# Moving two transposition steps and one wait inside the down product of a mixture-of-experts kernel

## What is computed

```
def swiglu(h, w_gu, w_down):
    gate, up = jnp.split(h @ w_gu, 2, axis=-1)
    return (jax.nn.silu(gate) * up) @ w_down

def moe_swiglu(h, router_w, w_gu, w_down):
    ...
    for e in range(N_EXPERTS):          # 8 experts, D_FF_E = 1408
        y = y + gates[..., e:e + 1] * swiglu(h, w_gu[e], w_down[e])
```

## Time and profile before

| | |
|---|---|
| median of 3 runs | 2287.32 us (2282.84 to 2290.6) |
| profiled execution | 2283.95 us, its span 2282.1 us |
| PE busy | 2029.0 us (89%) |
| DVE, ACT, POOL busy | 958.3, 725.9, 772.2 us |
| dense SwiGLU (layer 0) on PE | 873 to 1361 us |
| expert SwiGLU (layer 1) on PE | 1478.95 to 2224.6 us |
| HBM read, written | 284.45 MB, 32.65 MB |

### The profile page before, as it was taken

One profiled execution on the slowest core, in us unless ns is written; L12 is line 12 of the kernel. 1 busy time (PEld: TensorE's weight loads), 2 busy tenths in 40 slices (PEclk: granted clock), 3 DMA queues, 4 the chain that ended last, 5 costly groups with the idle time before them and its releaser, 6 DMA issues. The chain is left out here.

```text
span 2282.1 us, 38499 instructions
## 1 busy us (share of the span) xinstructions
PE 2029.0 (89%) x14354; PEld 1532.4 (67%) x14355; DVE 958.3 (42%) x1618; ACT 725.9 (32%) x1193; POOL 772.2 (34%) x474
## 2 busy tenths in 40 slices
PE   4998999999998798999999989399999899899990
PEld 2545776777676546878788867367776677677870
DVE  3203665666566355423222247353333433432226
ACT  0112332333233102222122201164445545544331
POOL 0006224422443112212121233275355645543324
PEclk7899999999999899999999998599999999999995
DMA  7113233223321514224322421586658758765344
GB/s 252 56 37 105 79 106 124 80 72 104 124 80 62 198 52 153 93 88 137 99 94 85 162 92 56 185 279 213 188 184 264 245 181 255 247 197 171 106 162 152
DMA packets 257563, 320.58 MB, mean 140 GB/s; under 512 B 25417, under 2 KB 197713, under 8 KB 257323
## 3 DMA queue, kind: packets, MB, share of 16 engines
q1 hardware_dynamic: 242315, 285.01, 39.0%
q10 hardware_dynamic: 10976, 17.49, 2.2%
q0 software_dynamic: 4032, 14.68, 1.8%
HBM read 284.45 MB, written 32.65 MB: 139 GB/s over the span
## 5 line engine op out<-in xcount | busy, mean ns | idle before, releaser
L1301 POOL TENSOR_TENSOR wlo<-wring,whi 128x1024 fp32r<-128x1024 f32 x182 | 461.0, 2536 | 781.7 <-ACT whi L1733 711.6
L1109 PE MATMUL pp<-whi,xTh 128*128 128x512 f32 (+1 forms) x1152 | 449.7, 390 | 37.5 <-issue 11.6
L1733 ACT ACTIVATE whi<-wring 128x1024 fp32r<-128x1024 f32 (+1 forms) x328 | 318.8, 980 | 454.8 <-PE pp L1111 375.2
L1111 PE MATMUL pp<-wlo,xTh 128*128 128x512 f32 (+1 forms) x1152 | 434.0, 377 | 0.0
L1110 PE MATMUL pp<-whi,xTl 128*128 128x512 f32 (+1 forms) x1152 | 433.6, 376 | 0.0
L2295 DVE TENSOR_TENSOR wlo<-wring,whi 128x1024 fp32r<-128x1024 f32 x182 | 227.3, 1249 | 229.4 <-ACT whi L1733 141.9
L1109 PEld LDWEIGHTS pp<-whi,xTh 128*128 128x128 f32 x1152 | 220.4, 191 | 93.3 <-issue 28.7
L1111 PEld LDWEIGHTS pp<-wlo,xTh 128*128 128x128 f32 x1152 | 219.9, 191 | 40.4
L1110 PEld LDWEIGHTS pp<-whi,xTl 128*128 128x128 f32 x1152 | 220.8, 192 | 34.9
L1109 PE MATMUL pp<-whi,hTh 128*128 128x512 f32 x528 | 212.7, 403 | 8.5 <-DVE ybuf L2251 3.9
L728 PE MATMUL pp<-xT,wring 128*128 128x512 f32 x384 | 206.5, 620 | 2.6 <-ACT scratch L1534 2.0
(11 more groups left out here) (291 smaller groups left out, 2675.0 us busy)
## 6 DMA issues: line engine op xcount, KB each, us to landing
wring<-in_moe_w_gu SPq DMA_DIRECT2D x320, 256.0 KB, 3.8
wring<-in_ada_w SPq DMA_DIRECT2D x80, 512.0 KB, 4.8
wring<-in_moe_w_down SPq DMA_DIRECT2D x160, 256.0 KB, 3.5
wring<-in_ffn_w_gu SPq DMA_DIRECT2D x80, 256.0 KB, 3.1
wring<-in_dn_w_in SPq DMA_DIRECT2D x96, 128.0 KB, 3.4
wring<-in_ffn_w_down SPq DMA_DIRECT2D x40, 256.0 KB, 3.0
expert_in<-zeros SPq DMA_DIRECT2D x36, 256.0 KB, 3.3
wring<-in_ada_w SPq DMA_DIRECT2D x32, 256.0 KB, 5.2
```

Of the source, the lines that this page charges most:

```text
L1109: pe.matmul(out, hi[:, c0 + c, tt], wh, start=(first and c == 0), stop=False)
L1111: mm = pe.matmul(out, hi[:, c0 + c, tt], wl, start=False, stop=(last and c == nk - 1))
L1301: pool.tensor_tensor(wlo[:, hs, 0:nk, 0:w], wring[:, ring_p.slot(k), 2:2 + nk, 0:w], whi[:, hs, 0:nk, 0:w].bitcast(F32), ALU.subtract).the ...
L1733: act.activation(whi[:, hs, 0:nk, 0:w], wring[:, ring_v.slot(k), 2 * s:2 * s + nk, 0:w], ACT.Copy)\
```

## The change

Three things, in the code of PE, ACT and DVE alike. PE waits before each of the halves 0 to 5 for `hTl` of that half's own chunk, where it waited before half 0 for chunks 0 to 4 and behind half 2 for chunk 5. The transposition of chunk 5 moves from half 1 to half 2. The groups of the next tokens move from halves 2, 3, 4, ... to halves 4, 6, 7, 8, then two behind each of 9, 10 and 11. POOL's order is untouched, and so is SP's.

```
+        TOKENS_AT = {4: [(0, 0)], 6: [(0, 1)], 7: [(1, 0)], 8: [(1, 1)], 9: [(2, 0), (2, 1)], 10: [(3, 0), (3, 1)],
+                     11: [(4, 0), (4, 1)]}
...
                             m = 6 * a + s
-                            if a == 0 and s == 0:
-                                pe.wait_ge(f["hTl_ready"], c * 6 + n * 5 + 1)
-                            after = (lambda t: h_group(c * 6 + n * 5 + t, 5, t)) if m == 1 else None
+                            if m < 6:
+                                pe.wait_ge(f["hTl_ready"], c * 6 + n * (m + 1) + 1)
+                            after = (lambda t: h_group(c * 6 + n * 5 + t, 5, t)) if m == 2 else None
...
-                            if m == 2:
-
+                            if m == 4:
                                 pe.wait_ge(f["hTl_ready"], c * 6 + n * 6 + 1)
...
-                            if m >= 2 and l:
-                                t2, g = (m - 2) // 2, m % 2
+                            for t2, g in TOKENS_AT.get(m, ()) if l else ():
...
                     for m in range(12):
+                        if m == 2:
+                            h_high(c * 6 + n * 5, n, 5)
                         high_after(24 + m, e, c, n)
-                        if m == 0:
-                            h_high(c * 6 + n * 5, n, 5)
```

More of the change, by code:

```diff
@@ L1851, in expert @@
                     for m in range(12):
+                        if m == 2:
+                            h_high(c * 6 + n * 5, n, 5)
                         high_after(24 + m, e, c, n)
-                        if m == 0:
-                            h_high(c * 6 + n * 5, n, 5)
-                        if m < 2 or l == 0:
+                        if l == 0:
                             continue
[L1857 to L1861, removed]
+                        for t2, g in TOKENS_AT.get(m, ()):
+                            if t2 == 0:
                                 xs_high(c + n, t2, g, 7)
+                            else:
+                                with act.If(n2 > t2):
+                                    xs_high(c + n, t2, g, 7)
                         if m in (5, 11):
@@ L2379, in expert @@
                                 add_y(e, m // 6, t)
[L2380 to L2385, removed]
+                        if l:
+                            for t2, g in TOKENS_AT.get(m, ()):
+                                if t2 == 0:
                                     xs_low(c + n, t2, g, 7)
+                                else:
+                                    with dve.If(n2 > t2):
+                                        xs_low(c + n, t2, g, 7)
                     return n2
```

## The result

| | before | changed |
|---|---|---|
| median of 20 runs each | 2284.85 us (2279.36 to 2292.06) | 2293.69 us (2289.54 to 2302.03) |
| ratio | 1 | 1.0038, 95% interval 1.003 to 1.0047 |
| profiled execution, its span | 2283.95, 2282.1 us | 2294.73, 2292.9 us |

A forecast was written before the change was run, and what follows sets the result against it. PE was taken as the bound, busy 2029.0 of 2282.1 us. Terms 3.0 + 0.5 + 0.5 + 0.5 + 2.4 = 6.9, so +7 us: execution 2283.95 to 2291, median 2294 (3.4 above the execution before), range 2286 to 2303.

The forecast's parts named there:

- What costs nothing: `hTl` waits, chunk 5's move and the dense layer: -0.5 to +1 us, taken as 0; experts 2, 4 and 7 also 0.
- The chain with the copies in it: With one tile, (1, 0) behind half 7 can't run until 5.25 us after ACT starts `whi` of half 9.
- Expert 0, forecast +3.0: Down product: (1, 0) waits about 2.5 us, PE ends 2.3 us later; with clock 3.0 (2.3 to 3.6).
- the clock term: Expert 0, after the wait at (1, 0): a clock fall costs some 1.3 us, taken with half its weight.
- Expert 1, forecast +0.5: Down product: a wait of 1.02 us at (1, 0), where one of 0.53 goes away: +0.5.
- Expert 6, forecast +2.4: +0.5 as in expert 1, then a 2.18 us wait between (2, 0) and (2, 1): +2.4, with fallen clock +3.7.
- Experts 3 and 5, forecast +0.5 each: Down products: PE 2.4 us late before the loop's jump; bounds 0 and 2.4 + 1.3 of clock, taken 0.5 each.
- The gap was to take all of it: Before experts 4 and 6: the gap counts from the jump, starts stay 6.5 and 6.8 us after the last wait.
- Rival 1: The gap at the loop's jump doesn't absorb and the clock falls: 10 to 16 us, 2297 to 2303; chance 0.22.
- Rival 2: Nothing: ACT comes through the copies faster, or PE's waits only move; -2 to +4 us, 2285 to 2291; chance 0.25.
- Rival 3: Faster: `xTl` waits in halves 3 to 5 go, no new ones come; at most -5.5 us, 2282; chance 0.08.
- The signs: `xTl` waits 12 to 18 us, singles 2 to 4; gaps before experts 4 and 6 about 3, starts near 6.5 behind.

The follow-up runs named there:

- waits_only: Kernel before with only PE's waits for `hTl` changed, each of halves 0 to 5 waiting for its own chunk: 2287.70 us, ratio 1.0005.
- groups_only: Kernel before with only the next tokens' groups moved to the later halves; chunk 5 and the `hTl` waits as before: 2295.19 us, ratio 1.0038.
- one_ahead: Changed kernel with group (0, 1) behind half 5 instead of 6, its `xTh` ahead of ACT's copies: 2292.26 us, ratio 1.0019 to the kernel before.
- before_unrolled: Kernel before with PE's expert loop alone written out as eight experts, so without its jump: 2284.52 us, ratio 0.9993.
- pair_spread: Changed kernel with (2, 0) behind half 9 and (2, 1) behind half 10 instead of both behind 9: 2291.45 us, ratio 1.0018 to the kernel before.
- last_at_8: Kernel before with (1, 1) behind half 8 instead of 5, and (2, 0), (2, 1) behind 9 and 10: 2285.04 us, ratio 0.9992.

## Why the prediction was right

The forecast of 2294 us met 2293.69. The mechanism and the places were right; that the number fits so closely is in part luck. The sum was +6.9 and 8.8 was measured, 1.9 too little; and the kernel before was taken at 2287.3, the median of three runs, where twenty give 2284.85, 2.5 too much. The two errors cancel, and so do several inside the sum.

**What costs nothing.** Right. waits_only is 1.0005, groups_only has the ratio of the whole change, and the dense layer, where only chunk 5 moves, keeps its length. The experts 2 and 4 cost nothing either, as forecast: their down products take 31.4 and 31.5 us, before 31.4 both (between (0, 0) and (0, 1) they have the halves 5 and 6, not half 5 alone as the prediction says). The -1.0 and +0.9 of their visits lie in gate and up.

**The chain with the copies in it.** Right where it was worked out: 5.22 us in expert 3 against 5.25, 5.58 in expert 0, where ACT waited a little longer for PE. one_ahead takes the copies out of this chain, and the wait behind half 7 of expert 3 goes. The chain's start held its place in the profiled execution (`whi` of half 9 comes 11.4 us into expert 0's down product, before 11.6), but not in that of groups_only (12.3), where it waited for its transfer.

**Expert 0, forecast +3.0.** Too small, the step being the clock term, which was taken "with half its weight". The down product is 3.9 us longer: 2.1 for the place of (1, 0), 0.3 for the chain, and 1.6 from the clock, which went to 1.2 GHz in full (7.34 instead of 5.7 us to the end). The table's +5.5 for the whole visit includes a gate and up part that was short in the one profiled execution of before (40.8 us; 41.7, 41.9 and 42.3 in before_unrolled, waits_only and the changed kernel). The pair with the loops written out gives +3.9 again.

**Expert 1, forecast +0.5.** +0.3 by the table, but not by this term: the wait at (1, 0) is 0.52 instead of 1.02, since PE came there later than the sum had it, and one of 0.53 went away, so the groups cost nothing here.

**Expert 6, forecast +2.4.** +1.4. The wait between (2, 0) and (2, 1) is 1.92 instead of 2.18, behind a wait of 0.80 at (1, 0), and the clock did not fall.

**Experts 3 and 5, forecast +0.5 each.** The totals, +0.4 and +0.6, are right for a reason that was half wrong. PE's lateness was taken as 2.4; it is 3.7 and 4.6 (down products of 24.7 and 25.4 us, before 21.0 and 20.9). In expert 3 the excess is 0.3 for a later `whi` of half 9, and 1.0 behind (1, 0), of which the largest part is a wait of 0.78 at (1, 1), behind DVE's low part of half 10, where 0.2 was taken. In expert 5, where the same sum gives 2.1, the excess is 0.7 for `whi` of half 9, behind a transfer that came late, and 1.8 behind (1, 0), where the clock fell to 1.2 GHz (below); the sum had no fall here.

The gap was to take all of it. It took 0.7 (4.97 to 4.23 us) and 2.3 (5.24 to 2.94). In expert 3 the next start came 8.3 us behind the last wait inside the loop (1807.65 to 1815.99); in expert 5 it came 10.6 us behind the last one (1974.02 to 1984.65). The distance was to stay at 6.5 and 6.8, so the reading that it is fixed failed. What is left, 3.0 and 2.3, stands against shorter gate and up products of the same experts: 40.3 and 40.7 us, before 42.9 and 42.4. These come ahead of the down product, so the gap behind it has no part in them. In expert 3 both traces run alike until ACT waits for weights, first the kernel before, then the changed one:

```profile
1764.31 1.06 ACT L1733 ACTIVATE whi<-wring 128x1024 fp32r<-128x1024 f32 x1 [4.08 <-DMA wring<-in_moe_w_gu]
...
1770.71 1.06 ACT L1733 ACTIVATE whi<-wring 128x1024 fp32r<-128x1024 f32 x1 [2.88 <-DMA wring<-in_moe_w_gu]
```

In the changed kernel these weights landed 1.2 us sooner after the product's start, PE waited 1.33 us for POOL where it had waited 2.50, and the fall of the clock behind that wait didn't come. It is more than one lucky trace: gate and up of the experts 0 to 6 take 391.1 to 393.0 us together in the four kernels with PE's loop and late groups (the changed one, groups_only, pair_spread, one_ahead) and 395.2 to 396.8 in the three others with PE's loop (before, waits_only, last_at_8). With both loops written out it is 383.2 before and 383.9 changed, no shorter. So with PE's loop some 4 us of the lateness are made up in gate and up, in expert 3 through weights that land sooner. Why they do was not tried. The prediction had no such term: it put the absorption in the gap alone, and there 3.0 of 8.3 us were absorbed. Without the loops' heads the two experts lose 4.8 and 5.3 us from start to start. The rule of the Trainium skill (Runtime: NRT & Kernel Launch, Instruction fetch mechanics), that a taken branch to a target outside the sequencer's window forces a fetch before execution goes on, agrees with the traces in kind: the gap of 4.97 us before expert 4 is gone in before_unrolled, which has no jump (1806.06, no wait). The prediction's step from it, that the two experts then cost 0 because the gap counts from a fixed point, doesn't agree with 8.3 and 10.6 us.

**Rivals.** Rival 1, the gap that doesn't absorb, describes the kernels with both loops written out: 13.0 us, inside its 10 to 16. Rival 2, nothing, fell with the ratio's interval. Rival 3 fell: the waits in the halves 3 to 5 did go in the experts 0 and 3, as it wanted, but ACT's copies kept their 1.95 us.

**The signs.** The waits for `xTl` rose to 12.7 us (12 to 18), with single ones up to 2.99 (2 to 4), at (1, 0) of the experts 0, 3 and 5. The gaps went to 4.2 and 2.9 us (about 3), but the starts did not stay near 6.5 us behind the last wait. The gap before expert 6 is named after DVE now:

```profile
1984.65 0.49 PE L1111 MATMUL pp<-whi,xTh 128*128 128x512 f32 x1 [2.94 <-DVE wlo L2295]
```

Of the 8.8 us, some 4 are in expert 0, about 1.5 in expert 6 and 1 in the experts 3 and 5. The rest, about 2, is in no place that more than one trace shows.

## What to carry to other kernels

Before moving a small step of an exchange between engines, write down in order what each engine does between two such steps in the new place: a copy that was harmless beside the chain costs its full length inside it, idle issue time too. A gap at one engine's loop head may lie beside a larger one at another's, so taking one of them away can measure as nothing and both as one per cent. And a forecast that meets the time can still hold terms that are wrong by a factor of nearly two: split the time by stage, and take the cover away in a further kernel, before calling it understood.

## What the runs showed of the hardware

**Loop heads.** ACT in the kernel before, at the heads of its second to fourth pass:

```profile
1649.19 1.28 ACT L1870 ACT_TABLE_LOAD   x1 [7.39 <-issue]
...
1814.24 1.28 ACT L1870 ACT_TABLE_LOAD   x1 [9.38 <-issue]
...
1981.63 1.28 ACT L1870 ACT_TABLE_LOAD   x1 [9.82 <-issue]
```

ACT is idle for 7.4 to 9.8 us ahead of each, and PE for about 5 at two of the three. Written out on PE alone the heads give 0.9993, on PE and ACT 0.9902, on DVE too nothing more that can be told.

**The clock after a wait.** The same wait of 1.92 us at the same group of expert 6 left the clock at 2.4 GHz in the changed kernel (matmuls of 0.39 us) and brought it to 1.2 GHz in one_ahead (0.63 us). In the changed kernel one of 2.29 did nothing in expert 3, and one of 2.31 at the same group of expert 5 was followed by matmuls of 0.63:

```profile
1974.02 0.66 PE L1075 MATMUL pp<-cm,x 128*128 128x128 f32 x4 [2.31 <-DVE xTl L2301]
...
1975.31 0.63 PE L1111 MATMUL pp<-whi,hTh 128*128 128x512 f32 x1
```

One of 2.82 in expert 5 of groups_only (at 1977.83) did nothing, one of 2.99 in expert 0 of the changed kernel brought the clock down. The length of the wait alone doesn't tell; a forecast for waits of about 2 to 3 us has to hold both cases.

**DVE beside POOL.** The low part of 128 x 1024 takes DVE 2.32 us where POOL has just begun another (DVE's at 1804.68, POOL's at 1804.63), and 1.23 us where POOL's next one starts only near the end of it (1820.30 in before_unrolled, with POOL's at 1821.29). It matters who is first: in the experts of the kernel before, 24 of DVE's 128 low parts of this size start while one of POOL's is running and take 1.76 us at the median (1.43 to 2.73); the other 104, most of which POOL joins later, take 1.21 to 1.35. The Trainium skill (GPSIMD Engine Reference, Specifications) says that GpSimd shares its SBUF interfaces with VectorE and contends with instructions that have two SBUF inputs, as this one has; the trace agrees for the instructions that start second. This length stands ahead of `xTl` on DVE; at 1.23 us instead, `xTl` could have started when its `xTh` was made (1806.11) instead of at 1806.92. By this estimate 0.8 us, the whole wait at (1, 1), is owed to it.
